# Expert stage of a two-block fp32 model: the last two of 32 expert pairs added from on-chip memory, the others gathered while these two run

## The chip, the cores and the metric

The program runs on one core of one Trainium2 chip, in fp32. The metric is the device time of one execution in microseconds (us). All figures of the trace come from one profiled execution.

## What is computed

The reference is a two-block network on 512 tokens of width 1024. Only its last part matters here: a mixture of 64 experts, two for each token, added to the residual, and a final normalisation.

```python
def _hier_moe(h, wg, bg, we, be, w_gate, w_up, w_down):
    ...
    gate_w = p_g * jax.nn.softmax(top_l, axis=-1)
    expert = g_idx * EXPERTS_PER_GROUP + top_i
    ...
    def expert_block(args):
        xb, e = args
        a = jax.nn.silu(xb @ w_gate[e]) * (xb @ w_up[e])
        return a @ w_down[e]

    y_pad = lax.map(expert_block, (x_pad.reshape(n_blocks, MOE_BLOCK, d), block_e)).reshape(rows, d)
    y = y_pad[dest] * w_s[:, None].astype(h.dtype)
    out = jax.ops.segment_sum(y, tok_s, num_segments=t)
...
        x = x + _hier_moe(hn, router_group_w[i], router_group_b[i], router_expert_w[i],
                          router_expert_b[i], expert_w_gate[i], expert_w_up[i], expert_w_down[i])
    return _rmsnorm(x, final_norm_g)
```

w_gate and w_up are 1024 x 512 for each expert, w_down is 512 x 1024: 6 MB an expert, some 400 MB in all, each read once.

## The kernel before

The engines' programs are written by hand, in the order in which they are to run, with semaphores between them; no scheduler moves anything. PE is TensorE, DVE VectorE, ACT ScalarE, POOL GpSimd, SP SyncE, which issues the weight loads.

The expert stage takes a little over the last third of the span. Experts are taken two at a time, as 32 **pairs**. A pair has 128 slots, 64 for each of its experts, of which on average 32 hold a token. The routing writes two tables: TAB has the token of each slot of a pair, DEST the row of y_d (a DRAM buffer of 1024 rows, one for each token and choice) for its result. An empty slot points outside the buffer and its row is skipped. For pair q:

- POOL gathers the token rows from hn_d (DRAM) into XG[q % 2] (L1893), and PE transposes them (L794). ACT copies the first half of the result to XT (L1162), DVE the second (L1779).
- PE multiplies by the gate weights (L804), 16 products of 64 x 512 results; ACT takes the tanh (L1166), DVE makes the gate from it (L1781). PE multiplies by the up weights (L804 too) and DVE finishes the product (L1784).
- PE transposes that (L811), ACT copies it (L1170), PE multiplies by the down weights (L821). DVE (L1788) and ACT (L1174) copy the two halves to YE, one buffer for all pairs, and POOL scatters YE to y_d (L1897). Pair q's copy waits until the scatter of pair q-1 has landed.

The weights come on SP's queue, 2 MB a load, six loads a pair, into a **ring** of nine slots of 2 MB. A load is issued when PE has ended the product that used its slot before. Slot names: the first four are WR[1], WR[2], WR[3] and WR[0]. PE's results go to eight PSUM banks in turn; a tile opens when the bank's last user has been read.

A general path (`more_rounds`) for experts with more than 64 tokens stands behind the pairs in every engine's program. It is not entered in the profiled execution: each engine loads the number of rounds into a register, compares, and goes on.

After the last scatter has landed, SP reads y_d back in eight loads (L2011), one for each block of 128 tokens and each of the two choices. DVE adds each, times its weight, to the residual X (L1796, 8 combines), ACT squares the rows (L1179) and takes the root (L1181), DVE makes the factor and multiplies the four row blocks by it and the gain `row` (L1800), and SP writes them out (L2014).

Of the kernel before, what the change touches and what calls it, by code (L numbers as in the profile page):

```python
# [14 lines left out]
P = 128  # L15
CAP = 64
PAIRS = 32
NONE = 4096
# [128 lines left out]
def program(nc, A, out):  # L147
    with ExitStack() as ctx:
# [160 lines left out]
        RR, OK, o2 = zl(2, 4), zl(2, 4), zl(2, 4)  # L309
# [13 lines left out]
        YG = [view(zone, ring0 + 1024 * n, 1024) for n in range(8)]  # L323
# [15 lines left out]
        plan += [(("ex", n), RING[n % NRING]) for n in range(6 * PAIRS)]  # L339
        W = Slots(plan)  # L340
        EW = [A[n].rearrange("e (p t) n -> e p (t n)", p=P) for n in ("eg", "eu", "ed")]
# [19 lines left out]
        def tensor_program(pe):  # L361
# [409 lines left out]


            pe_plan(pe, T, any_bank())
            for q in range(PAIRS):
                pe_pair(pe, T, q, lambda n: loaded("ex", 6 * q + n), lambda n: slot("ex", 6 * q + n), any_bank, ("gather", q % 2, 16 * (q // 2 + 1)))
                for n in range(6):
                    W.ended[("ex", 6 * q + n)] = (("g", q), ("g", q), ("u", q), ("u", q), ("d", q, 1), ("d", q, 1))[n]
            pe.wait_ge(S("rounds"), 1)

        def pe_plan(pe, table, b):  # L780
# [4 lines left out]
            ins.then_inc(table.f("tab"), 1)  # L785

        def pe_pair(pe, table, q, ready, weight, bank, gathered):
# [10 lines left out]
            for mat, name in enumerate(("g", "u")):  # L798
                o = open_tile(pe, (name, q), bank(), 1, table)
# [13 lines left out]
            pe.wait_ge(*table.free("at", q))  # L813
            pe.wait_ge(*ready(4))
# [15 lines left out]
        def scalar_program(act):  # L830
# [35 lines left out]
            odd_columns(0, sm("n1"))  # L866
            act.wait_ge(S("lam"), 1)
# [278 lines left out]
            act.wait_ge(S("hn_rows"), 4)  # L1146
            act.dma_start(row, A["fn2"].partition_broadcast(P)).then_inc(S("row"), 16)
# [6 lines left out]

            for q in range(PAIRS):
                act_pair(act, T, q, q % 2)

        def act_pair(act, table, q, par):
# [11 lines left out]
            act.activation(aT, table.ap("at", q).rearrange("p (a b) -> p a b", a=4), ACT.Copy).then_inc(table.s("at", q), 1)  # L1170
            act.wait_ge(*table.full("d", q, 1))
            if q:
                act.wait_ge(S("y_st"), 16 * q)
            act.activation(YE[:, 512:1024], table.ap("d", q, 1), ACT.Copy).then_inc(table.s("d", q, 1), 1)  # L1174

        def act_end(act):
            for i in range(4):
                act.wait_ge(S("comb"), 2 * i + 2)
# [7 lines left out]
        def vector_program(dve):  # L1186
# [564 lines left out]

            for q in range(PAIRS):
                dve_pair(dve, T, q, q % 2)

        def dve_plan(dve, own, table):
# [12 lines left out]
            step(dve.tensor_tensor(OK, OK, ck("tok").rearrange("p (a b) -> p a b", a=2), ALU.mult))  # L1768
            step(dve.tensor_tensor(BM[:, 0, :, :], BM[:, 0, :, :], bc(OK[:, 0, :], 2, 32), ALU.mult))
            dve.tensor_tensor(BM[:, 1, :, :], BM[:, 1, :, :], bc(OK[:, 1, :], 2, 32), ALU.mult).then_inc(S("am"), 1)  # L1770
# [3 lines left out]

        def dve_pair(dve, table, q, par):
            dve.wait_ge(*table.full("xt", q, 1))
            if q > 1:
                dve.wait_ge(*table.full("u", q - 2))
            dve.tensor_copy(XT[par][:, 4:8, :], table.ap("xt", q, 1).rearrange("p (a b) -> p a b", a=4)).then_inc(table.s("xt", q, 1), 1)  # L1779
            dve.wait_ge(S("a_tanh"), q + 1)  # L1780
            dve.scalar_tensor_tensor(AT, AT, 1.0, table.ap("g", q), ALU.add, ALU.mult).then_inc(table.s("g", q), 1)  # L1781
            dve.wait_ge(*table.free("g", q))
            dve.wait_ge(*table.full("u", q))
            dve.scalar_tensor_tensor(AT, AT, 0.5, table.ap("u", q), ALU.mult, ALU.mult).then_inc(table.s("u", q), 1)  # L1784
            dve.wait_ge(*table.full("d", q, 0))
            if q:
# [460 lines left out]
```

## Time and profile before

| | us |
|---|---|
| median of 3 runs | 2759.55 |
| lowest, highest | 2752.46, 2761.93 |
| profiled execution, its time | 2755.31 |
| profiled execution, its span | 2753.5 |
| PE busy (share of the span) | 2396.7 (87%) |
| DVE, ACT, POOL busy | 595.7, 330.1, 161.1 |

The span runs from the first instruction of the program to the last. The profile's page cuts it into 40 slices of 69 us. In the last 14 slices DMA is busy at nine tenths or more and moves some 425 GB/s: the expert weights. In the last slice this falls to four tenths. "PEclk" is the granted clock of TensorE, 1.00 for the full 2.4 GHz and 0.50 for 1.2 GHz. Views used: the chain of waits (what each step of the end waited for), windows (busy time in a stretch), the timeline (instructions in order), groups by line, and the DMA view. A line of the trace is a line of the kernel as printed above.

### The profile page before, as it was taken

The page shows a single profiled execution, that of the slowest core. Times are in us where ns is not written, and L with a number is a line of the kernel's source. Part 1 is how long each engine was busy: PE and PEld are TensorE (multiplying, and loading weights), DVE is VectorE, ACT ScalarE, POOL GpSimd, SP SyncE. Part 2 cuts the span into 40 slices and gives each one's busy share as a digit, 9 for nine tenths or more (in the row PEclk, how much of TensorE's full clock was granted, in tenths as well). Part 3 has the DMA queues.
Part 4 walks back from the last instruction along what each step waited for, and adds up shares of the span by engine and source line. Part 5 has one row for each costly group of instructions (what it writes and reads, how often), then busy time and mean ns, then how long its engine had stood idle before and what let it go on. Part 6 is the DMA issues. An engine that isn't in the chain of part 4 may idle for free.

```text
span 2753.5 us, 20729 instructions
## 1 busy us (share of the span) xinstructions
PE 2396.7 (87%) x8540; PEld 1131.7 (41%) x8540; DVE 595.7 (22%) x1191; ACT 330.1 (12%) x637; POOL 161.1 (6%) x149
## 2 busy tenths in 40 slices
PE   7998989897999999997999998698788878888874
PEld 3654544453444554443564444333233323332331
DVE  1144252523144223002152111211000000010002
ACT  2012122210021110002111000000000000000001
POOL 0000000000004330000000000000000000000000
PEclk9998999898999999998978999799999999999997
DMA  4210000002222322212632223699999999999994
GB/s 181 79 59 31 31 31 31 16 23 99 88 111 93 110 95 85 85 68 74 113 94 92 115 95 131 244 425 426 426 425 426 426 425 426 425 425 414 427 425 180
DMA packets 68416, 549.00 MB, mean 199 GB/s; under 512 B 20961, under 2 KB 25185, under 8 KB 36449
## 3 DMA queue, kind: packets, MB, share of 16 engines
q1 hardware_dynamic: 42384, 518.11, 46.4%
q10 hardware_dynamic: 16720, 21.13, 2.7%
q0 software_dynamic: 9216, 8.42, 0.9%
q8 instruction: 69, 1.13, 0.2%
q14 instruction: 27, 0.21, 0.0%
HBM read 540.76 MB, written 32.01 MB: 208 GB/s over the span
## 4 chain that ended last, share of the span: by engine, by line
PE 61%; DMA 20%; DVE 6%; ACT 2%; issue 1%; ACTq 1%; DVEq 0%; POOL 0%; SPq 0%; POOLq 0%
PE ps L364 23%; DMA sb<-in_eu 14%; PE ps L804 9%; PE ps L643 8%; PE ps L419 6%; DMA sb<-in_eg 5%; PE ps L821 4%; PE ps L538 2%; PE ps L703 1%; PE ps L508 1%; PE ps L530 1%; DMA sb<-in_ed 1%; DVE sb L1190 1%; PE ps L509 1%; DVE sb L1312 1%
## 5 line engine op out<-in xcount | busy, mean ns | idle before, releaser
L364 PE MATMUL ps<-sb 128*128 128x512 f32 (+2 forms) x1920 | 792.8, 575 | 33.5 <-DVE sb L1322 15.3
L804 PE MATMUL ps<-sb 128*64 128x512 f32 x2048 | 495.6, 640 | 116.9 <-DMA sb<-in_eu 87.7
L364 PEld LDWEIGHTS ps<-sb 128*128 128x128 f32 x1920 | 360.5, 195 | 449.4 <-issue 431.0
L804 PEld LDWEIGHTS ps<-sb 128*64 128x64 f32 x2048 | 180.3, 146 | 410.3 <-issue 381.9
L821 PE MATMUL ps<-sb 128*64 128x512 f32 x1024 | 233.6, 610 | 24.9 <-ACT sb L1170 19.9
L419 PE MATMUL ps<-sb 128*128 128x512 f32 x512 | 251.3, 621 | 0.0
L643 PE MATMUL ps<-sb 128*128 128x512 f32 x512 | 220.0, 592 | 0.8 <-ACT sb L856 0.8
L643 PEld LDWEIGHTS ps<-sb 128*128 128x128 f32 x512 | 97.3, 190 | 122.9 <-issue 122.9
L821 PEld LDWEIGHTS ps<-sb 128*64 128x64 f32 x1024 | 73.6, 139 | 162.8 <-issue 136.0
L1190 DVE TENSOR_TENSOR sb<-sb 128x32 f32<-128x32 f32 (+10 forms) x259 | 106.7, 430 | 133.6 <-PE ps L609 83.2
L419 PEld LDWEIGHTS ps<-sb 128*128 128x128 f32 x512 | 93.0, 199 | 80.1 <-issue 79.6
L1784 DVE SCALAR_TENSOR_TENSOR sb<-sb,ps 128x512 f32<-128x512 f32 x32 | 22.1, 690 | 314.9 <-PE ps L804 314.9
L856 ACT ACTIVATE sb<-ps 128x512 f32<-128x512 f32 (+6 forms) x123 | 60.1, 499 | 229.0 <-PE ps L364 92.5
L538 PE MATMUL ps<-sb 128*64 128x128 f32 x320 | 51.8, 295 | 39.3 <-ACT sb L856 25.2
L1897 POOL DMA_INDIRECT y_d<-sb x32 | 32.2, 1007 | 891.5 <-ACT sb L1174 862.8
L1223 DVE COPY sb<-ps 128x512 f32<-128x512 f32 (+7 forms) x65 | 36.5, 561 | 210.7 <-PE ps L364 96.9
L1781 DVE SCALAR_TENSOR_TENSOR sb<-sb,ps 128x512 f32<-128x512 f32 x32 | 22.1, 690 | 255.5 <-ACT sb L1166 255.5
L538 PEld LDWEIGHTS ps<-sb 128*64 128x64 f32 x320 | 35.2, 143 | 83.6 <-issue 33.1
L1170 ACT ACTIVATE sb<-ps 128x512 f32<-128x512 f32 x32 | 19.1, 598 | 389.0 <-PE ps L811 389.0
L371 PE MATMUL ps<-sb 128*128 128x128 f32 x128 | 23.1, 366 | 47.2 <-DVE sb L1213 23.7
L974 ACT ACTIVATE sb<-ps,sb 128x128 f32<-128x128 f32 (+3 forms) x64 | 33.2, 523 | 242.3 <-DVE sb L1397 239.3
L1788 DVE COPY sb<-ps 128x512 f32<-128x512 f32 x32 | 22.2, 693 | 177.8 <-PE ps L821 177.8
(233 smaller groups left out, 1461.2 us busy)
## 6 DMA issues: line engine op xcount, KB each, us to landing
sb<-in_eg SPq DMA_DIRECT2D x64, 2048.0 KB, 32.5
sb<-in_eu SPq DMA_DIRECT2D x64, 2048.0 KB, 34.1
sb<-in_ed SPq DMA_DIRECT2D x64, 2048.0 KB, 32.5
sb<-in_m SPq DMA_DIRECT2D x16, 2048.0 KB, 7.4
sb<-in_winF SPq DMA_DIRECT2D x6, 2048.0 KB, 9.9
sb<-in_mg SPq DMA_DIRECT2D x8, 1536.0 KB, 6.6
sb<-in_mgg SPq DMA_DIRECT2D x4, 2048.0 KB, 7.2
sb<-in_wo SPq DMA_DIRECT2D x4, 2048.0 KB, 7.2
```

Of the source, the lines that this page charges most:

```text
L364: ins = pe.matmul(out, lhsT, rhs, start=k == 0, stop=k == len(pieces) - 1)
L419: ins = pe.matmul(o, lhsT, rhs, start=k == 0, stop=k == 7)
L508: pe.matmul(o[:, 0:nk], qT[hs, j, 128 * i:128 * i + 128], kT[hs, ty, 0:nk], start=True, stop=False)
L538: ins = pe.matmul(ob[hs, 128 * i:128 * i + 128], Vn[:, kb, 128 * ty + 64 * h:128 * ty + 64 * h + 64], PTR[ty][:, 128 * kb:128 * kb + 128], ...
L643: ins = pe.matmul(acc[2 * i + nh], HT[:, k, 128 * i:128 * i + 128], w[:, q, 512 * nh:512 * nh + 512], start=k == 0, stop=k == 31)
L804: ins = pe.matmul(o[64 * e:64 * e + 64, :], x[:, k, 64 * e:64 * e + 64], weight(2 * mat + e)[:, 512 * k:512 * k + 512], start=k == 0, stop ...
L821: ins = pe.matmul(o[64 * e:64 * e + 64, :], aT[:, k, 64 * e:64 * e + 64], weight(4 + e)[:, d:d + 512], start=k == 0, stop=k == 3)
L856: act.activation(dst, T.ap(*name) if src is None else src, ACT.Copy).then_inc(T.s(*name), 1)
L974: act.activation(PR[n % 2][:, ty, 0:nk], T.ap("s", n, ty)[:, 0:nk], ACT.Exp, bias=ST[n % 2][:, ty:ty + 1], scale=0.125, accum_out=ST[n % 2 ...
L1190: return own(dve.tensor_tensor(o, a, b, op))
L1223: dve.tensor_copy(dst, T.ap(*name) if src is None else src).then_inc(T.s(*name), 1)
L1897: pool.indirect_dma_start(out=y_d, out_offset=bass.IndirectOffsetOnAxis(ap=rows, axis=0), in_=YE, in_offset=None, bounds_check=1023, oob_i ...
```

## The change

Pairs 0 to 29 (`ENDS = 30`) still go through y_d. Pairs 30 and 31 do not: their YE is made with the routing weight already in it (WTAB, one column for each), and PE spreads it over the tokens by products with one-hot matrices OH (`pe_spread`: 8 products of 128 x 128 by 128 x 512 a pair, one for each block of 128 tokens and half of the width). DVE adds these to X (`dve_spread`, 8 additions a pair).

The results of the 30 pairs are no longer loaded by SP. POOL gathers them from y_d in eight gathers of 128 rows (GY, the rows' table, leaves out those of pairs 30 and 31), after the scatter of pair 29 has landed; DVE combines six of them behind its XT copy of pair 31, and two behind the up product of pair 31. For their buffers they take WR[1], the two XG and `row`. The gain `row` is thus loaded later: ACT issues that load after the sixth combine. The last 12 loads of weights leave WR[1] out and go round the other eight slots. The two last loads, the down weights of pair 31, are issued as 8 loads of 512 KB, and PE's products with them go by k, both halves of the width together. At the end DVE makes the row blocks 2 and 3, POOL and ACT make blocks 0 and 1. Early in the program, two DMAs on ACT's queue fill y_d with x.

```diff
@@ the ring
-        YG = [view(zone, ring0 + 1024 * n, 1024) for n in range(8)]
+        OH = [view(CKt, 128, 4, 128), view(RW, 0, 4, 128)]
+        YA = [view(WR[1], 1024 * n, 1024) for n in range(4)] + [XG[0], row, XG[1], view(WR[1], 0, 1024)]
...
-        plan += [(("ex", n), RING[n % NRING]) for n in range(6 * PAIRS)]
+        plan += [(("ex", n), RING[n % NRING]) for n in range(6 * ENDS)]
+        plan += [(("ex", n), RING[1 + (n - 6 * ENDS) % (NRING - 1)]) for n in range(6 * ENDS, 6 * PAIRS)]
@@ TensorE
+            o = open_tile(pe, ("wtab",), any_bank())
+            pe.wait_ge(S("bw"), 1)
+            for n in range(8):
+                ins = pe.matmul(o[:, 0:2], AM[:, n // 4, n % 4, :], BW[:, n, :], start=n == 0, stop=n == 7)
...
+        def pe_spread(pe, q, bank):
+            pe.wait_ge(S("oh"), 4 * (q - ENDS) + 4)
+            pe.wait_ge(*T.free("d", q, 0))
+            pe.wait_ge(*T.free("d", q, 1))
+            for i in range(4):
+                for nh in range(2):
+                    o = open_tile(pe, ("sp", q, i, nh), bank())
+                    pe.matmul(o, OH[q - ENDS][:, i, :], YE[:, 512 * nh:512 * nh + 512], start=True, stop=True).then_inc(T.f("sp", q, i, nh), 1)
...
             for mat, name in enumerate(("g", "u")):
+                if q == PAIRS - 1 and mat == 1:
+                    pe_spread(pe, q - 1, bank)
...
+            if q == PAIRS - 1:
+                both = [open_tile(pe, ("d", q, nh), bank(), 1, table) for nh in range(2)]
+                for k in range(4):
+                    for e in range(2):
+                        pe.wait_ge(S(f"last{e}{k}"), 16)
+                    for nh in range(2):
+                        for e in range(2):
...
@@ ScalarE
+            for c in range(2):
+                act.dma_start(y_d[512 * c:512 * c + 512, :], A["x"]).then_inc(S("y_init"), 16)
...
-            act.wait_ge(S("hn_rows"), 4)
-            act.dma_start(row, A["fn2"].partition_broadcast(P)).then_inc(S("row"), 16)
...
             for q in range(PAIRS):
                 act_pair(act, T, q, q % 2)
+                if q == ENDS:
+                    act.wait_ge(S("comb"), 6)
+                    act.dma_start(row, A["fn2"].partition_broadcast(P)).then_inc(S("row"), 16)
...
+            if q == PAIRS - 1:
+                act.activation(e1, e1, ACT.Sqrt, scale=0.0)
...
+            act.wait_ge(S("l_r"), 1)
+            for i in range(2):
+                act.wait_ge(S("gained"), i + 1)
+                act.activation(Z[:, i, :], Z[:, i, :], ACT.Copy, scale=r5[:, i:i + 1]).then_inc(S("fin_a"), 1)
@@ VectorE
+            dve_pair(dve, T, ENDS, 0)
+            q = PAIRS - 1
+            dve_xt(dve, T, q, 1)
+            for n in range(6):
+                dve_comb(dve, n, S("comb"), YA[n], S(f"comb{n}"))
+            dve_gate(dve, T, q)
+            dve_spread(dve, q - 1, own)
+            dve_up(dve, T, q)
...
+            for n in (6, 7):
+                dve_comb(dve, n, S("comb"), YA[n], S(f"comb{n}"))
+            dve_ye(dve, T, q)
+            dve_spread(dve, q, own)
...
+        def dve_spread(dve, q, own):
...
+                    dve.tensor_tensor(xs, xs, T.ap("sp", q, i, nh), ALU.add).then_inc(S("xadd") if q > ENDS else T.s("sp", q, i, nh), 1)
@@ GpSimd
+            pool.wait_ge(S("y_st"), 16 * ENDS)
+            pool.wait_ge(S("gy"), 1)
+            for n in range(8):
...
+                gather(pool, YA[n], y_d, GY[:, n % 2, n // 2:n // 2 + 1], 1023, S(f"comb{n}"))
+            pool.wait_ge(S("xadd"), 8)
...
+        def pool_end(pool):
+            pool.wait_ge(S("row"), 48)
+            for i in range(2):
+                pool.wait_ge(S("l_sq"), i + 1)
+                pool.tensor_tensor(Z[:, i, :], X[:, i, :], row, ALU.mult).then_inc(S("gained"), 1)
@@ SyncE
+            for k in range(4):
+                for e in range(2):
+                    sp.dma_start(slot("ex", 6 * PAIRS - 2 + e)[:, 1024 * k:1024 * k + 1024],
+                                 EW[2][2 * PAIRS - 2 + e][:, 1024 * k:1024 * k + 1024]).then_inc(S(f"last{e}{k}"), 16)
...
-            sp.wait_ge(S("y_st"), 16 * PAIRS)
-            for n in range(8):
-                i, c = n // 2, n % 2
-                sp.dma_start(YG[n], y_d[512 * c + 128 * i:512 * c + 128 * i + 128, :]).then_inc(S(f"comb{n}"), 16)
```

On ACT, around the end of pair 30, before: the four operations of pair 30, then those of pair 31.

```order
L1162 ACTIVATE sb<-ps 128x512 [waits full2,full5]
L1166 ACTIVATE sb<-ps 128x512 [waits full2,full7]
L1170 ACTIVATE sb<-ps 128x512 [waits full4,full1]
L1174 ACTIVATE sb<-ps 128x512 [waits y_st,full3]
L1162 ACTIVATE sb<-ps 128x512 [waits full1,full4]
L1166 ACTIVATE sb<-ps 128x512 [waits full1,full6]
L1170 ACTIVATE sb<-ps 128x512 [waits full3,full0]
L1174 ACTIVATE sb<-ps 128x512 [waits y_st,full2]
```

And now (L1202, L1206, L1210 and L1220 are the same four; in_fn2 is the gain):

```order
L1202 ACTIVATE sb<-ps 128x512 [waits full3,full6]
L1206 ACTIVATE sb<-ps 128x512 [waits full3,full0]
L1210 ACTIVATE sb<-ps 128x512 [waits full5,full2]
L1220 ACTIVATE sb<-ps,sb 128x512 [waits free3,y_st,full4]
L1196 DMA sb<-in_fn2 128x1024 [waits comb]
L1202 ACTIVATE sb<-ps 128x512 [waits full2,full5]
L1206 ACTIVATE sb<-ps 128x512 [waits full2,full7]
L1210 ACTIVATE sb<-ps 128x512 [waits full4,full1]
L1212 ACT_TABLE_LOAD
L1212 ACTIVATE sb<-sb 128x4
L1220 ACTIVATE sb<-ps,sb 128x512 [waits full7,full3]
```

The load of the gain, with its wait on the combines, now stands ahead of ACT's copy to XT of pair 31, and the square root's table is loaded ahead of pair 31's last copy.

On DVE, pair 31 before, from its copy to XT to its copy to YE:

```order
L1779 COPY sb<-ps 128x512 [waits full1,full5]
L1781 SCALAR_TENSOR_TENSOR sb<-sb,ps 128x512 [waits a_tanh]
L1784 SCALAR_TENSOR_TENSOR sb<-sb,ps 128x512 [waits full7,free6]
L1788 COPY sb<-ps 128x512 [waits y_st,full1]
L2071 TENSOR_LOAD sb [waits rounds]
```

And now, from the same copy to the first of the additions for pair 30 (L1835 is a combine, L1903 the gate):

```order
L1899 COPY sb<-ps 128x512 [waits full2,full6]
L1835 SCALAR_TENSOR_TENSOR sb<-sb 128x1024 [waits comb0]
L1835 SCALAR_TENSOR_TENSOR sb<-sb 128x1024 [waits comb,comb1]
L1835 SCALAR_TENSOR_TENSOR sb<-sb 128x1024 [waits comb,comb2]
L1835 SCALAR_TENSOR_TENSOR sb<-sb 128x1024 [waits comb,comb3]
L1835 SCALAR_TENSOR_TENSOR sb<-sb 128x1024 [waits comb,comb4]
L1835 SCALAR_TENSOR_TENSOR sb<-sb 128x1024 [waits comb,comb5]
L1903 SCALAR_TENSOR_TENSOR sb<-sb,ps 128x512 [waits a_tanh]
L1848 TENSOR_TENSOR sb<-sb,ps 128x512 [waits full0,comb]
```

Six combines, each of which waits for its own gather, stand between the copy to XT and the gate of pair 31.

## Rows read from the trace of the kernel before

**Rows 1.** Chain that ended last, from 2600 us: start, duration (us), what.

```profile
2683.55 31.33 DMA sb<-in_ed
...
2723.71 2.60 DMA y_d<-sb
...
2726.33 0.34 SPq L2011
```

**Rows 2.** Windows: stretch, length, busy us (PE, PEld, DVE, ACT, POOL), PEclk, DMA, GB/s.

```profile
2700.00:2710.00 10.00, 8.44 (x41) 3.11 (x39) 0.69 (x1) 0.60 (x1) 0.00 (x0) 1.00 0.30 126
2710.00:2720.00 10.00, 7.91 (x40) 3.32 (x38) 1.38 (x2) 0.60 (x1) 0.00 (x0) 1.00 0.09 38
```

**Rows 3.** Timeline of pair 31: start, duration (us), engine, line, out<-in, [idle before].

```profile
2695.34 0.60 ACT L1162 ACTIVATE sb<-ps 128x512 f32<-128x512 f32 x1
2695.79 0.69 DVE L1779 COPY sb<-ps 128x512 f32<-128x512 f32 x1 [3.82 <-PE ps L794]
...
2696.58 7.09 PE L804 MATMUL ps<-sb 128*64 128x512 f32 x32 [0.83 <-ACT sb L1162]
...
2704.34 0.69 DVE L1781 SCALAR_TENSOR_TENSOR sb<-sb,ps 128x512 f32<-128x512 f32 x1 [7.86 <-ACT sb L1166]
...
2705.23 7.09 PE L804 MATMUL ps<-sb 128*64 128x512 f32 x32 [1.56 <-DMA sb<-in_eu]
...
2712.43 0.69 DVE L1784 SCALAR_TENSOR_TENSOR sb<-sb,ps 128x512 f32<-128x512 f32 x1 [7.40 <-PE ps L804]
...
2714.02 0.60 ACT L1170 ACTIVATE sb<-ps 128x512 f32<-128x512 f32 x1 [9.72 <-PE ps L811]
...
2715.13 7.09 PE L821 MATMUL ps<-sb 128*64 128x512 f32 x32 [1.15 <-DMA sb<-in_ed]
```

**Rows 4.** Timeline of the end.

```profile
2733.32 8.23 DVE L1796 SCALAR_TENSOR_TENSOR sb<-sb 128x1024 f32<-128x1024 f32 x6 [0.60 <-DMA sb<-y_d]
...
2741.58 1.06 ACT L1179 ACTIVATE sb<-sb 128x1024 f32<-128x1024 f32 x1 [1.63 <-DVE sb L1796]
...
2742.75 1.28 ACT L1181 ACT_TABLE_LOAD   x1
...
2745.29 4.87 DVE L1800 SCALAR_TENSOR_TENSOR sb<-sb 128x1024 f32<-128x1024 f32 x4
2746.60 3.92 SPq L2014 DMA_DIRECT2D out<-sb  x4
```

**Rows 5.** Timeline of POOL: a scatter to y_d, a gather from hn_d.

```profile
2664.08 1.01 POOL L1897 DMA_INDIRECT y_d<-sb  x1 [29.46 <-ACT sb L1174]
...
2665.39 1.02 POOL L1893 DMA_INDIRECT sb<-hn_d,sb  x1 [0.31 <-issue]
```

**Rows 6.** DMA view from 2660 us: issues, count, median us from issue to landing.

```profile
y_d<-sb POOLq DMA_INDIRECT x3, 10.1
sb<-hn_d,sb POOLq DMA_INDIRECT x1, 14.3
```

**Rows 7.** Page, part 3: a queue's packets, MB, share of 16 DMA engines, whole span.

```profile
q0 software_dynamic: 9216, 8.42, 0.9%
```

**Rows 8.** DMA view of 2640 to 2664 us: all packets.

```profile
DMA packets 876, 10.15 MB, mean 423 GB/s; under 512 B 230, under 2 KB 230, under 8 KB 265
```

**Rows 9.** DMA view of 2731 to 2739 us: q1's packets, MB, share of 16 engines.

```profile
q1 hardware_dynamic: 807, 2.92, 91.6%
```

**Rows 10.** Windows, TensorE after an idle stretch: the columns of rows 2.

```profile
1762.20:1768.00 5.80, 4.91 (x16) 2.69 (x18) 0.69 (x1) 0.60 (x1) 0.00 (x0) 0.50 0.09 26
```

**Rows 11.** Windows, TensorE at the start: length, PE busy us (count), PEclk, DMA share, GB/s.

```profile
22.50:75.40 52.90, 52.90 (x124) 1.00 0.18 72
```

**Rows 12.** Source view of L2071, register load of the rounds: durations (ns), start.

```profile
L2071 POOLq TENSOR_LOAD <-sb x1: 475/475/475, 2726.3 to 2726.3; - x1
```

**Rows 13.** Groups by line, POOL: line, op, out<-in (shapes) xcount | busy us, mean ns.

```profile
L1845 POOL TENSOR_TENSOR sb<-sb 128x512 f32<-128x512 f32 x32 | 48.8, 1525 | 22.1 <-DVE sb L1554 14.5 <-DVE sb L1558 7.6
L1832 POOL TENSOR_TENSOR sb<-sb 128x512 f32<-128x512 f32 x32 | 33.3, 1039 | 224.7 <-ACT sb L1015 224.7
```

More of the change, by code:

```diff
@@ L17 @@
 PAIRS = 32
+ENDS = 30
 NONE = 4096
@@ L1749, in vector_program @@
             dve_plan(dve, own, T)
-            for q in range(PAIRS):
-                dve_pair(dve, T, q, q % 2)
+            flat8 = HI.rearrange("p a b -> p (a b)")
+            after(tt(o2, OK, WT, ALU.mult))
+            after(tt(BW, bc(ck("iota")[:, ENDS:PAIRS], 1, 8), bc(flat8, 2, 2), ALU.is_equal))
+            dve.tensor_tensor(BW, BW, bc(o2.rearrange("p a b -> p (a b)"), 2, 2), ALU.mult).then_inc(S("bw"), 1)
+            dve_rows(dve, own, ENDS)
+            copy(("wtab",), WTAB, T.ap("wtab")[:, 0:2])
@@ L1755, in dve_plan, with dve_hots @@
+        def dve_hots(dve, own):
+            dve.wait_ge(*T.full("rank"))
+            dve.wait_ge(*T.full("lg"))
+            dve.wait_ge(*T.free("tab"))
+            dve.wait_ge(own.sem, own(dve.tensor_copy(TOKF, TAB[:, ENDS:PAIRS])))
+            for p in range(2):
+                for i in range(4):
+                    dve.tensor_scalar(OH[p][:, i, :], ck("iota"), TOKF[:, p:p + 1], -128.0 * i, ALU.subtract, ALU.is_equal).then_inc(S("oh"), 1)
         def dve_plan(dve, own, table):
@@ L1880, in gpsimd_program @@
             pool.wait_ge(S("hn"), 16)
-            for q in range(PAIRS + 2):
+            for q in range(PAIRS):
+                if q == 2:
+                    pool.wait_ge(S("y_init"), 32)
                 if q > 1:
@@ L1997, in sync_program @@
                     sp.wait_ge(*T.full("lg"))
-                load(("ex", n), EW[k // 2][2 * q + k % 2])
+                if n < 6 * PAIRS - 2:
+                    load(("ex", n), EW[k // 2][2 * q + k % 2])
+            for e in range(2):
+                sp.wait_ge(*T.full(*W.ended[W.before[("ex", 6 * PAIRS - 2 + e)]]))
+            for k in range(4):
+                for e in range(2):
+                    sp.dma_start(slot("ex", 6 * PAIRS - 2 + e)[:, 1024 * k:1024 * k + 1024],
+                                 EW[2][2 * PAIRS - 2 + e][:, 1024 * k:1024 * k + 1024]).then_inc(S(f"last{e}{k}"), 16)
         def sync_more(sp):
@@ L2067, in meet, with nothing, more_rounds @@
                 eng.sem_clear(S("go" + letter))
-        def more_rounds(eng, letter, more, pair):
+        def nothing(eng):
+            pass
+        def more_rounds(eng, letter, more, pair, tail=nothing):
             eng.wait_ge(S("rounds"), 1)
@@ L2083, in more_rounds @@
                     eng.reg_add(k, k, 1)
+                tail(eng)
+                meet(eng, letter)
                 eng.reg_add(r, r, 1)
```

141 lines of the change are left out of this document (111 added, 30 removed).

## The prediction, made before the changed kernel was run

> **What bounds the kernel now.** I read the chain that ended last first, for what holds the end; then the windows of the last pair, for who is busy; then the timeline, for the hand-offs that the change moves. The chain says that the pairs hang on their weights: the last load is issued at 2683.55 and lands 31.33 us later, at 2714.9 [rows 1]. The windows refine this. From 2700 to 2710 the 16 DMA engines are only 0.30 busy, from 2710 to 2720 only 0.09 [rows 2]: most engines have ended and a few still carry their share of the last loads. A load has landed only when the slowest engine has done its part. I call these the slow engines; everything new that is put on them before 2714.9 counts. Behind the weights come 7.1 us of down products, a scatter, the reads of y_d, six combines in 8.23 us and the final normalisation [rows 1, 3, 4], 31 us from the end of the last product to the end of the span. The change goes at this tail.
>
> **Removed.** The last scatter and the reads of y_d, from 2723.71 on [rows 1], and the combines behind them, up to 2741.55 [rows 4]. Most of this goes to other places, so I don't subtract it; I lay out the new end from pair 31 on and compare the ends.
>
> **What comes ahead of pair 31's gate products.** PE needs both copies to XT. DVE's is unmoved. ACT's (0.60 us [rows 3]) now stands behind the load of the gain, which waits for six combines, and these for six gathers. So the question of the case is when the sixth gather lands.
>
> The scatter of pair 29 is issued at 2664.08 and lands about 10.1 us later, at 2674.1; the gather behind it, issued at 2665.39, takes 14.3 us, to 2679.7 [rows 5, 6]. That is 5.6 us for one indirect DMA whose rows are mostly empty. It has 9216 / 64 = 144 packets, 9 for each DMA engine [rows 7]. A 16 KB packet of weights takes 16384 B over 423 / 16 GB/s = 0.62 us [rows 8], and 9 x 0.62 = 5.6: each packet of POOL's queue waits out one packet of SP's. The Trainium skill ("DMA: Bandwidth & Descriptors", section "Queues, rings and completion order") has each engine alternate between its queues, a whole packet of some 9 to 17 descriptors at a time; the 5.6 us fit turns of either length, and both give the same landing here.
>
> The eight new gathers are full: their rows are 4 KB, and a 4 KB packet takes 0.16 us (2.92 MB / 807 packets over 365 GB/s / 0.916 / 16 [rows 9]). 15 rows in 16 belong to the 30 pairs, so a gather costs a loaded engine 9 x 0.62 + 7.5 x 0.16 = 6.8 us. They are issued from 2674.2, one in 1.3 us [rows 5], and queue behind the gather that lands at 2679.7. If all weights came in 16 KB packets, the sixth would land at 2679.7 + 6 x 6.8 = 2720.4, which is the late bound. But the last two loads now come in 4 KB packets. At 2679.7 a slow engine has 35.2 / 0.62 = some 56 packets of weights left; 40 of them stay at 16 KB and take 40 x 0.62 + 33 x 0.16 = 30.1 us with the packets in between, to 2709.8. By then 40 of the 54 packets of six gathers are through; the last 14 alternate with 4 KB packets, 14 x 0.31 = 4.3 us. **The sixth gather lands at 2714.1.** The early bound comes from DVE: it starts to combine after its XT copy, at 2696.5, and six combines at 8.23 / 6 = 1.37 us [rows 4] end at 2704.7. I take 2714.1, since the 5.6 us are measured under the very same load; both bounds stay for the range.
>
> **The path from there.** Sixth combine to 2715.4; issue of the gain's load (0.34 to 0.4, like SP's issue [rows 1]) and ACT's copy 0.6, with hand-offs 2716.6. PE starts the gate products there and not at 2696.58 [rows 3]: 20.0 us later.
> - Gate products 7.09 us at full clock. PE has been idle for 20 us by then. After an idle stretch the granted clock was 0.50 from 1762.2 to 1768.0, with PE busy [rows 10]; half of 5.8 us is lost, 2.9 (bounds: 0, and 7.1 if all of it runs at 1.2 GHz). To 2726.6.
> - Spread of pair 30, 8 products. A product of 128 x 128 by 128 x 512 takes 52.90 / 62 = 0.85 us at full clock (two records each) [rows 11]: 6.8 us, to 2733.4. Its eighth tile takes the bank of the gate products, which DVE frees in time (tanh and gate, from 2703.67 to 2705.03, take 1.4 us [rows 3]). DVE's eight additions, 0.7 us each like L1784, run beside it.
> - Up products 7.1, to 2740.5. Then L1784, transposes, L1170: 2712.32 to 2714.62, 2.3 us [rows 3], to 2742.8. The two remaining combines and the root's table lie under what follows.
> - Down products 7.1, to 2749.9. The weights don't hold them: the slow engines carry at most 8 gathers x 1.3 us = 10.2 us more than before, so the last part lands by 2725. The finer loads are thus worth nothing here; with the old order they would have been worth up to three quarters of 7.1 us.
> - Scaled copy 0.7; spread of pair 31, 6.8; last addition 0.7: 2758.1.
> - The last square, 1.06 and its read 0.19, is one way on; then the table (still loaded: the program has a table load between squares and root on this path too), root and DVE's small steps, 2742.75 to 2745.29, to 2761.9; two final products on DVE at 1.2 us [rows 4] to 2764.3. The other way is POOL. It waits for the eighth addition, loads the number of rounds (0.5 us for the load itself [rows 12]; I take 1 us with the branch) and makes two products of 128 x 1024. Its 128 x 512 ones take 1.04 to 1.53 us [rows 13], so 2.1 to 3.1 each; at 2.5 it ends at 2764.1, and ACT's scaling, 1.06 as for a square [rows 4], at 2765.2. POOL is the later. The last write is issued there.
> - Before, the last final product ended at 2750.16 (2745.29 + 4.87 [rows 4]) and the span at 2753.5: 3.3 us. New end 2768.5, **15 us later**.
>
> **At nothing.** The 8 MB of traffic that fill y_d: at 423 GB/s [rows 8] 20 us, when PE is busy all of 52.90 us and DMA at 0.18 [rows 11]; without that cover a load that PE waits for would come up to 20 us late. The nine small DVE steps and eight products behind the routing: they run while the first gather is under way, some 3.4 us of cover, and could cost 1 us. One slot less for the last 12 loads: a load waits 32 us or so in the queue [rows 1], a slot is 5; only fast engines run dry, and no one waits for those. The one-hot matrices, eight small DVE steps in pair 2: DVE idles 7 us and more at a time [rows 3].
>
> **Rivals.**
> - *Early gathers.* The sixth gather lands before DVE wants it; the combines end at 2704.7 and all follows 10.7 us sooner: span 2757.9, 4.4 us over before, which is no difference that can be told. For it: twelve of the 16 engines have spare time [rows 2], and the slow ones may give POOL's queue more turns. Against: 5.6 us for nine nearly empty packets [rows 6, 7]. It decides at a landing of 2707: sooner than that, the loss is under 0.3%. The Trainium skill (the same page, section "Anatomy of one DMA — SWDGE (gpsimd) path") gives about 2.0 us plus the bytes over 436 GB/s for a DMA from GpSimd, some 3.2 us for 512 KB; by that all six are in by 2684, which is this rival. The trace shows that figure only on idle queues (2.60 us for a scatter [rows 1]), not under the weights (10.1 [rows 6]).
> - *Late gathers.* The 4 KB loads give no extra turns: 2720.4, 6.3 us more, span 2774.8.
> - *Faster.* ACT's copy would go ahead without the combines, as if the gain's load stood elsewhere. Gate products at 2696.6, spread to 2710.5, up to 2717.6, down from 2719.9 to 2727.0, then as above 18.6 us: 2745.6, 8 us less. Against it stands the order of ACT, and DVE's gate is behind the same combines. Only if the gathers were in by 2700 and the additions cheaper than I think is anything of it left.
>
> **The numbers.** My forecast 0.56, late gathers 0.20, early 0.20, faster 0.04. From the profiled execution (2755.31, of which 2753.5 span) the forecast is +15.0. The median of the runs stands 4.2 us above that execution; I add to the median: 2759.6 + 15.0 = 2774.6. Early gathers give 2764.0, late ones 2780.9. With the clock (-2.9 to +4.2), POOL's products (1 us either way) and the spread of the runs, the range is 2760 to 2784. About 0.3%, 8.3 us, is what a measurement of this kernel can tell from no change. Forecast and late case lie above, but the forecast's low flank reaches it: slower 0.76. Early gathers and that flank: same 0.20. Faster 0.04.
>
> **What would show it.** In the profile after: PE idle between the transposes of pair 31 and its gate products, some 20 us, ended by ACT's copy; DVE's fourth to sixth combine each waiting for its gather, 3 to 7 us apart; gathers from y_d with 12 to 35 us to landing; the down products of pair 31 back to back, with no wait for in_ed. Wrong would be: combines back to back at 1.37 us from 2696 on (early gathers), a gap of 25 us and more (late), gate products that start before the sixth combine (the path is not the one I laid out), or a pace of the earlier pairs that has changed.

## The result, and the profile after

The kernel before took 2756.24 us (median of 6 runs, 2751.08 to 2761.93), the changed kernel 2772.45 us (6 runs, 2770.28 to 2776.36). The ratio is 1.0061 with a 95% interval of 1.0045 to 1.0077: **16.2 us slower**, about twice what a measurement can tell. Forecast was +15.0 us and 2774.6 us, range 2760 to 2784. (The forecast added to the 2759.55 us of the first three runs of the kernel before; with six its median is 3.3 us lower.) The profiled execution of after took 2771.85 us, its span is 2770.1 (before 2753.5).

The first view is again the chain that ended last, from the scatter of pair 29 on (start, duration in us, what):

```profile
2662.09 10.31 DMA y_d<-sb
...
2679.63 30.96 DMA sb<-y_d,sb
...
2710.62 1.30 DVE sb L1835
...
2711.93 0.36 ACTq L1196
...
2712.39 0.61 ACT sb L1202
...
2713.05 9.73 PE ps L828 x32
2722.78 7.07 PE ps L807 x16
...
2739.24 7.12 PE ps L846 x32
```

Before, the chain at this place was a load of weights that landed at 2714.9 and then the scatter and the reads of y_d [rows 1]. Now it is the scatter of pair 29, a gather that takes 30.96 us to land, the sixth combine (L1835), the issue of the gain's load (L1196), ACT's copy to XT (L1202) and the products of pair 31. No weights stand in it.

The timeline shows the same hand-offs with the idle time before each (columns as in rows 3):

```profile
2694.23 4.06 DVE L1835 SCALAR_TENSOR_TENSOR sb<-sb 128x1024 f32<-128x1024 f32 x3
...
2702.57 1.28 DVE L1835 SCALAR_TENSOR_TENSOR sb<-sb 128x1024 f32<-128x1024 f32 x1 [4.28 <-DMA sb<-y_d,sb]
2708.11 1.28 DVE L1835 SCALAR_TENSOR_TENSOR sb<-sb 128x1024 f32<-128x1024 f32 x1 [4.25 <-DMA sb<-y_d,sb]
2710.62 1.28 DVE L1835 SCALAR_TENSOR_TENSOR sb<-sb 128x1024 f32<-128x1024 f32 x1 [1.23 <-DMA sb<-y_d,sb]
...
2712.39 0.60 ACT L1202 ACTIVATE sb<-ps 128x512 f32<-128x512 f32 x1 [19.17 <-DVE sb L1835]
...
2713.05 9.73 PE L828 MATMUL ps<-sb 128*64 128x512 f32 x32 [19.46 <-ACT sb L1202]
...
2739.24 7.10 PE L846 MATMUL ps<-sb 128*64 128x512 f32 x32 [0.69 <-ACT sb L1210]
```

Three combines find their rows there, three wait for a gather each. ACT idles 19.17 us before its copy, PE 19.46 us before the gate products, which started at once in [rows 3] (0.83 us, at 2696.58). The down products (L846) wait 0.69 us, for ACT, where they waited 1.15 us for in_ed before.

The windows of the same stretch (columns of rows 2):

```profile
2700.00:2710.00 10.00, 0.00 (x0) 0.00 (x0) 2.57 (x2) 0.00 (x0) 0.00 (x0) 0.50 0.64 253
2710.00:2720.00 10.00, 6.96 (x20) 2.14 (x22) 1.28 (x1) 0.60 (x1) 0.00 (x0) 0.58 0.37 150
```

In [rows 2] PE was busy 8.44 us of the first ten; now it does nothing there, and the clock granted is 0.50, the lower of the two levels (1.2 GHz). DMA is busier than before, 0.64 in place of 0.30: the gathers share the engines with the last weights. The DMA view from 2662 to 2700 us answers [rows 6]:

```profile
sb<-y_d,sb POOLq DMA_INDIRECT x8, 19.7
y_d<-sb POOLq DMA_INDIRECT x1, 10.3
sb<-hn_d,sb POOLq DMA_INDIRECT x1, 14.4
```

And the timeline of the end, which answers [rows 4]:

```profile
2756.46 1.28 ACT L1228 ACT_TABLE_LOAD   x1
...
2756.52 4.63 POOL L2070 TENSOR_TENSOR sb<-sb 128x1024 f32<-128x1024 f32 x2 [58.76 <-ACT sb L1226]
...
2757.99 0.18 DVE L1935 RECIPROCAL sb<-sb 128x4 f32<-128x4 f32 x1 [1.35 <-ACT sb L1228]
2758.21 0.67 DVE L1936 TENSOR_TENSOR sb<-sb 128x4 f32<-128x4 f32 x1
2758.91 2.26 DVE L1938 TENSOR_TENSOR sb<-sb 128x4 f32<-128x4 f32 x1
...
2761.61 2.19 ACT L1232 ACTIVATE sb<-sb 128x1024 f32<-128x1024 f32 x2 [3.65 <-DVE sb L1940]
2761.61 2.48 DVE L1926 SCALAR_TENSOR_TENSOR sb<-sb 128x1024 f32<-128x1024 f32 x2
2762.92 1.53 SPq L2176 DMA_DIRECT2D out<-sb  x2
2764.51 1.36 SPq L2179 DMA_DIRECT2D out<-sb  x2
```

**How the traces are compared from here on.** The scatter of pair 29 starts at 2664.08 before and at 2662.09 after, and elsewhere in the experiments too (2662.08 in e1, 2666.68 in e2): executions drift by a few us ahead of the stretch that matters. The pairs themselves are not changed, from the first gather of rows to this scatter it is 905.3 us before and 905.4 after. So I count from the start of that scatter in each trace. Before ends 89.4 us behind it (2753.5 - 2664.1), after 108.0 (2770.1 - 2662.1): 18.6 us more, of which the 2.0 us by which the scatter came sooner are to be taken off to get the difference of the two spans, 16.6. In the eleven traces of this study the scatter starts between 2661.0 and 2668.4, so these 2.0 us can't be laid to the change. Medians of runs decide on the size; the trace says where it lies.

### The profile page after: what moved, and what is told of

It reads as the page before. It is cut to its first block, busy times and chain, and to the rows that moved or that the text cites. A ratio compares the mean times of both kernels' runs of the same rounds, so it can differ in the third digit from the quotient of the medians.

```text
span 2770.1 us, 20900 instructions
## 1 busy us (share of the span) xinstructions
PE 2420.0 (87%) x8588; PEld 1144.4 (41%) x8588; DVE 609.9 (22%) x1223; ACT 335.4 (12%) x642; POOL 172.7 (6%) x157
## 3 DMA queue, kind: packets, MB, share of 16 engines
q8 instruction: 70, 1.15, 0.2%
## 4 chain that ended last, share of the span: by engine, by line
PE 62%; DMA 19%; DVE 6%; ACT 2%; issue 2%; ACTq 1%; POOL 0%; DVEq 0%; POOLq 0%
PE ps L371 22%; DMA sb<-in_eu 13%; PE ps L828 10%; PE ps L650 8%; PE ps L426 6%; PE ps L858 5%; DMA sb<-in_eg 2%; PE ps L545 2%; PE ps L710 1%; PE ps L515 1%; PE ps L537 1%; DMA sb<-in_ed 1%; DMA sb<-y_d,sb 1%; DVE sb L1241 1%; PE ps L516 1%
## 5 line engine op out<-in xcount | busy, mean ns | idle before, releaser
L371 PE MATMUL ps<-sb 128*128 128x512 f32 (+2 forms) x1920 | 790.6, 573 | 32.6 <-DVE sb L1373 15.3
L1241 DVE TENSOR_TENSOR sb<-sb 128x32 f32<-128x32 f32 (+11 forms) x261 | 107.0, 428 | 133.8 <-PE ps L616 83.2
L1903 DVE SCALAR_TENSOR_TENSOR sb<-sb,ps 128x512 f32<-128x512 f32 x32 | 22.1, 690 | 260.9 <-ACT sb L1206 260.9
L1210 ACT ACTIVATE sb<-ps 128x512 f32<-128x512 f32 x32 | 19.1, 598 | 368.2 <-PE ps L835 368.2
```

Of the source, the lines that this page charges most:

```text
L371: ins = pe.matmul(out, lhsT, rhs, start=k == 0, stop=k == len(pieces) - 1)
L1241: return own(dve.tensor_tensor(o, a, b, op))
```

## The experiments

My theory: two orders of instructions make the loss. ACT's load of the gain, with its wait for six combines, stands ahead of ACT's copy to XT; and on DVE the six combines stand ahead of the gate. Both hang on the sixth gather, which is late because it shares the DMA engines with the weights. Rival one: the loss is in the weights themselves, which the gathers push back. Rival two: it is in the new work on the path (16 products that spread, 16 additions, the POOL and ACT share of the last step), and the wait would be hidden without them.

### The gain's load behind pair 31 (e1_gain_last)

```diff
-                if q == ENDS:
-                    act.wait_ge(S("comb"), 6)
-                    act.dma_start(row, A["fn2"].partition_broadcast(P)).then_inc(S("row"), 16)
...
+            act.wait_ge(S("comb"), 6)
+            act.dma_start(row, A["fn2"].partition_broadcast(P)).then_inc(S("row"), 16)
```

The added lines stand behind the last step of pair 31 on ACT; nothing else is changed.

> The load of the gain is issued behind all of ACT's work for pair 31; all else as in the changed kernel. My theory: ACT's copy to XT waits on the six combines only through this load. Gate products start at about 2694.4 in place of 2713.05 and end near 2701.5; then DVE's gate, behind the sixth combine, becomes the wait (2712.6), the eighth tile of the spread follows, up products 2713.4 to 2720.5. That is 16 us less: about 2756 us, span about 2754. Rival, the slow engines' weights hold the end anyway: then less than 5 us are won, and PE waits for in_ed.

Measured: 2757.11 us (median of 10), ratio to the kernel before 1.0009 [0.9993, 1.0025]; **15.3 us less than the changed kernel**, where 16 were expected. From the scatter to the end 93.2 us in place of 108.0. The timeline of PE and DVE:

```profile
2693.87 7.09 PE L828 MATMUL ps<-sb 128*64 128x512 f32 x32 [2.39 <-DMA sb<-in_eg]
...
2709.25 1.28 DVE L1834 SCALAR_TENSOR_TENSOR sb<-sb 128x1024 f32<-128x1024 f32 x1 [1.09 <-DMA sb<-y_d,sb]
2710.45 0.68 DVE L1902 SCALAR_TENSOR_TENSOR sb<-sb,ps 128x512 f32<-128x512 f32 x1
...
2711.19 2.08 PE L807 MATMUL ps<-sb 128*128 128x512 f32 x2 [4.02 <-DVE sb L1902]
2713.20 8.91 PE L828 MATMUL ps<-sb 128*64 128x512 f32 x32
```

The gate products no longer wait for the combines, only 2.39 us for their weights, and take 7.09 us, at full clock. Now the second order bites: the gate (L1902) follows the sixth combine, the last two products of the spread wait 4.02 us for it, and the up products take 8.91 us in place of 7.09 because PE had stood still (granted clock 0.79 from 2713.2 to 2722.1). So the wait on ACT costs 15 us net of what the second wait takes back. Rival two falls: all the new work is still there. Rival one falls as the main cause: by it less than 5 us could be won, and the down products wait 0.69 us for ACT, not for weights.

### DVE's combines behind the gate (e2_combines_late)

The gain's load as in the run before, and on DVE:

```diff
-            for n in range(6):
-                dve_comb(dve, n, S("comb"), YA[n], S(f"comb{n}"))
...
+            for n in range(6):
+                dve_comb(dve, n, S("comb"), YA[n], S(f"comb{n}"))
```

The removed lines stand ahead of the gate of pair 31, the added ones behind the step that follows its up products; the additions of pair 30 no longer wait for the combines, those of pair 31 do.

> As e1_gain_last, and DVE makes the gate, the additions of pair 30 and the up product of pair 31 first, then combines 0 to 5, the scaled copy, combines 6 and 7. My theory: no one in pair 31 waits for a gather any more. Gate products to 2701.5, spread to 2708.5, up products to 2715.6, down products held by their last parts (about 2723) to 2725; last addition 2734.5, end near 2749: 21 us less than the changed kernel, 2751 to 2752 us, and 4 to 5 below the kernel before. Rival, DVE's combines only move and become the wait ahead of the copy to YE: no more than e1_gain_last, 2756.

Measured: 2752.20 us (10), ratio 0.9983 [0.9970, 0.9995], where 2751 to 2752 us were expected; from the scatter to the end 86.2 us, 7.0 less than e1. In the timeline PE has no gap from the gate products to the end of the up products, and the six combines run back to back, since all rows are in by then:

```profile
2698.55 7.09 PE L828 MATMUL ps<-sb 128*64 128x512 f32 x32 [2.38 <-DMA sb<-in_eg]
2705.57 7.14 PE L807 MATMUL ps<-sb 128*128 128x512 f32 x16
...
2712.64 7.09 PE L828 MATMUL ps<-sb 128*64 128x512 f32 x32
...
2720.45 8.23 DVE L1835 SCALAR_TENSOR_TENSOR sb<-sb 128x1024 f32<-128x1024 f32 x6
```

The books close in the traces: 108.0 - 14.8 - 7.0 = 86.2, against 89.4 before. **The two waits cost 21.8 us, and what the change takes off the tail is worth 3.2 us net of the work it adds.** What remains of rival one is the 2.38 us wait for in_eg ahead of the gate products; [rows 3] had 0.83 there, for ACT. Counted from the scatter, though, the gate products start no later than before: at 31.9 us, and at 32.5 in the kernel before.

That the gathers are late because of the weights shows in the eighth of this run. It is issued when nearly all weights have landed (SP's queue takes 4.6% of the engines' time from 2722 to 2724), and lands in 4.6 us, where the sixth, the same 512 KB, took 29.2:

```profile
sb<-y_d,sb POOLq DMA_INDIRECT x1, 4.6
```

### The last two loads whole (e3_whole_loads)

The changed kernel with its last two loads in one 2 MB piece each, as before. PE waits for both whole loads ahead of the down products instead of for each piece; all other waits stay:

```diff
-                for e in range(2):
-                    sp.dma_start(slot("ex", 6 * PAIRS - 2 + e)[:, 1024 * k:1024 * k + 1024],
-                                 EW[2][2 * PAIRS - 2 + e][:, 1024 * k:1024 * k + 1024]).then_inc(S(f"last{e}{k}"), 16)
+                load(("ex", n), EW[k // 2][2 * q + k % 2])
```

> The two last loads of weights are again 2 MB each, in 16 KB packets, all else as in the changed kernel. If POOL's queue gets one packet for each packet of SP's, the sixth gather lands later: from 4.3 us for 14 turns beside 4 KB packets to 14 x 0.62 + 13 x 0.16 = 10.8, so 6 us later (2716 to 2717 in place of 2710.6), and the time is 5 to 6 us more, about 2778. If the engines share by bytes, the landing and the time don't change.

Measured: 2778.62 us (4), ratio 1.0081 [1.0064, 1.0098], 6.2 us more than the changed kernel in the medians; 3.0 more from the scatter to the end of the profiled one. The combines in its timeline:

```profile
2700.70 1.28 DVE L1836 SCALAR_TENSOR_TENSOR sb<-sb 128x1024 f32<-128x1024 f32 x1 [2.16 <-DMA sb<-y_d,sb]
2705.97 1.28 DVE L1836 SCALAR_TENSOR_TENSOR sb<-sb 128x1024 f32<-128x1024 f32 x1 [3.99 <-DMA sb<-y_d,sb]
2711.96 1.28 DVE L1836 SCALAR_TENSOR_TENSOR sb<-sb 128x1024 f32<-128x1024 f32 x1 [4.70 <-DMA sb<-y_d,sb]
2717.98 1.28 DVE L1836 SCALAR_TENSOR_TENSOR sb<-sb 128x1024 f32<-128x1024 f32 x1 [4.74 <-DMA sb<-y_d,sb]
```

The gathers land 5.3, 6.0 and 6.0 us apart to the end, where in the changed kernel the sixth came 2.5 us behind the fifth. Counted from the scatter the sixth combine starts 52.8 us later here (2717.98 - 2665.18), 48.5 in the changed kernel (2710.62 - 2662.09): 4.3 us sooner by the finer loads, two thirds of the 6.3 that I had worked out. At the end 3.0 of them are left, because the gate products, behind 25.18 us of idle time, took 8.56 us here and 9.73 in the changed kernel. The finer loads help the gathers, and through them the kernel, though they were not cut for that.

### All final products on DVE (e4_dve_final)

The changed kernel, with the four final products on DVE as before and none on POOL and ACT:

```diff
-            for i in (2, 3):
+            for i in range(4):
...
-                pool_end(pool)
```

> The four final products are all on DVE again and are written out in the order of before; no work on POOL and no scaling on ACT at the end. In the changed kernel's trace two small DVE steps of 128 x 4 took 0.67 and 2.26 us while POOL ran its product, against 0.16 before. If POOL's products hold DVE, the two steps are back at 0.16 to 0.2, 2.6 us are won and 2.4 us of two more final products are lost, and ACT's 1.1 us behind them go: 0 to 1.5 us less, 2771 to 2772. If not, the steps stay slow and the time is 1 to 3 us more.

Measured: 2772.04 us (4), ratio 1.0057 [1.0040, 1.0074]: by the medians of four and six runs no difference from the changed kernel can be told. The traces tell one: from the last addition to the end 12.0 us here and in e10 below, and 14.8 or 14.9 in all five traces with POOL's share (after, e1, e2, e3, e7). Its timeline:

```profile
2760.62 0.16 DVE L1932 TENSOR_TENSOR sb<-sb 128x4 f32<-128x4 f32 x1
2760.81 0.16 DVE L1934 TENSOR_TENSOR sb<-sb 128x4 f32<-128x4 f32 x1
...
2761.41 4.87 DVE L1922 SCALAR_TENSOR_TENSOR sb<-sb 128x1024 f32<-128x1024 f32 x4
2762.72 3.92 SPq L2172 DMA_DIRECT2D out<-sb  x4
```

The two small DVE steps take 0.16 us each; with POOL's products beside them they took 0.67 and 2.26, which is 2.6 of the 2.8 us. The run takes ACT's products away together with POOL's, but ACT's start only when these steps have ended, so they can't be what held them. Sharing the last step among three engines is a loss, not a gain.

### Whole loads without the two waits (e7_late_whole)

e2 with the last two loads whole, the edit of e3, its wait of PE for both loads too.

> e2_combines_late with the two last loads whole again. If finer loads are worth what the prediction's text gave them once nothing else holds the down products: the second whole load lands at about 58 us after the scatter of pair 29 (2722.9 in e3_whole_loads at 2665.2 for the gathers that end with it), the down products start there and not at 55.4: 2 to 3 us slower than e2_combines_late, about 2754.5 us. If the engines' queues are done before, no difference.

Measured: 2754.95 us (10), ratio 1.0001 [0.9990, 1.0013]; 2.75 us more than e2, but the two were run beside other runs of the kernel before (medians 2755.20 and 2754.26). From the scatter to the end 87.0 against 86.2. Its down products wait for the load:

```profile
2720.11 7.11 PE L847 MATMUL ps<-sb 128*64 128x512 f32 x32 [1.33 <-DMA sb<-in_ed]
```

With the two waits gone the finer loads take this 1.33 us down to 0.69, a wait for ACT; they are worth 0.8 us in the traces; the medians say 2.8, but the intervals of the two ratios overlap. In the changed kernel they did nothing for the down products, which came 16 us behind the last weights.

### The parts put together, and the gathers held back (e5_best, e8_gathers_later)

e5 is e2 and e4 together, and the spread and the last down products in the other order, half a row first, so that the squares can start sooner:

```diff
-                for k in range(4):
-                    for e in range(2):
-                        pe.wait_ge(S(f"last{e}{k}"), 16)
-                    for nh in range(2):
+                for nh in range(2):
+                    for k in range(4):
+                        for e in range(2):
+                            if nh == 0:
+                                pe.wait_ge(S(f"last{e}{k}"), 16)
```

> e2_combines_late and e4_dve_final together, and the down products of pair 31 again one half of the width after the other, so that the first half's scaled copy and its spread can start while the second half is multiplied. From the scatter of pair 29 to the end the profile of before has 89.4 us, of e2_combines_late 86.2. My theory: the final products on DVE take 2.8 us off (14.8 to 12.0 from the last addition to the end, as in e4_dve_final), the halves 0.9: 82.4, 7 us under the kernel before, about 2748 us, ratio 0.9975. Rival, the end hangs on the last weights' landing (2723.3 in e2_combines_late): the halves win nothing and the down products wait 1 to 2 us, 84.5, ratio 0.998 to 0.999.

Measured: 2752.53 us (12), ratio 0.9993 [0.9984, 1.0001], 85.9 us from the scatter: missed by some 4 us. The way from the last addition to the end took 12.6, not less than the 12.0 of e4: the squares of all rows fall together behind the last half. And the last addition came at 73.3 us, after 71.4 in e2, since pair 31 as a whole came later: its gate products waited for their weights until 34.4 us and not 31.9. Up to there e5 and e2 run the same code, so this is the spread between two executions. The next run asked whether the gathers are what holds the weights. It is e5 with one wait moved:

```diff
-                    pool.wait_ge(*T.full("u", ENDS - 2))
+                    pool.wait_ge(*T.full("xt", ENDS + 1, 1))
```

POOL now issues the gathers from y_d only when pair 31 has been transposed, some 19 us later.

> e5_best with the first gather from y_d held until the transposes of pair 31 have ended, some 17 us later, so that the slow engines do the weights for the gate and up products of pair 31 first. If the gathers only take turns from the weights: gate products start 2.4 us sooner (PE waited so long for in_eg in e2_combines_late), all weights land at the same time as before or 1 us sooner, the sixth combine ends some 10 us later, near the scaled copy: 0 to 2 us less than e5_best. Rival, the combines now hold the scaled copy: 2 to 5 us more than e5_best.

Measured: 2748.20 us (12), ratio 0.9979 [0.9966, 0.9991], 83.4 us from the scatter. The gate products start at 30.3 us with a shorter wait (34.4 in e5, 31.9 in e2). But the halves now show their price, since the first half of the down products needs every piece of both loads:

```profile
2692.79 7.09 PE L831 MATMUL ps<-sb 128*64 128x512 f32 x32 [1.50 <-DMA sb<-in_eg]
...
2720.94 4.51 PE L850 MATMUL ps<-sb 128*64 128x512 f32 x20 [1.46 <-DMA sb<-in_ed]
```

### The gathers held back, rows in the order of the change (e8_again, e10_later_rows)

The same kernel once more, and beside it e10, which is e2 and e4 with the gathers held back and without the halves.

> The same kernel as e8_gathers_later, to set beside e10_later_rows on one chip: 83.4 us from the scatter of pair 29 to the end, ratio to the kernel before 0.998. If its first result owed more than 2 us to the chip or the moment, it comes out at 0.999 or above.

> e8_gathers_later with the down products, the spread and the additions of pair 31 again in the changed kernel's order (by k, then by row block). In e5_best the squares of all four row blocks bunched behind the last four additions and cost 0.6 us (12.6 from the last addition to the end, 12.0 in e4_dve_final), and the halves won 0.7 us between down products and spread. So both should cancel: within 1 us of e8_gathers_later's 83.4 us from the scatter of pair 29 to the end, about 2748.5 us. If the last weights hold the down products (e8_gathers_later waited 1.5 us for in_ed after three eighths of them), the order by k waits later and less: 1 us better.

Measured: e8_again 2750.49 us (12), ratio 0.9984 [0.9974, 0.9994], 83.2 us from the scatter; e10 2749.06 us (12), ratio 0.9980 [0.9967, 0.9993], 82.0 us, 1.2 to 1.4 less than the kernel with the halves, as expected of weights that hold the down products. The two can't be told apart by their times. Both are faster than the kernel before by about 0.2%, with intervals clear of 1, in e8's first result as well, though this is less than the 0.3% that the prediction gave a single comparison. Against the changed kernel it is 0.8%. The timeline of e10:

```profile
2691.47 7.09 PE L828 MATMUL ps<-sb 128*64 128x512 f32 x32 [1.52 <-DMA sb<-in_eg]
...
2715.01 7.10 PE L846 MATMUL ps<-sb 128*64 128x512 f32 x32 [0.69 <-ACT sb L1209]
```

The down products need not wait for weights, and the wait ahead of the gate products is down from 2.38 (e2) to 1.52 us. e10 ends 4.2 us sooner from the scatter than e2: 1.4 up to the last addition (70.0 us and 71.4), and 2.8 behind it (12.0 and 14.8), POOL's share of the last step. The 1.4 us stand at the start of the gate products already: 30.0 to 30.5 us in the three traces with the gathers held back, 31.8 to 34.4 in the four with early gathers whose gate products wait for weights (e1, e2, e5, e7). The groups don't overlap, but the second spreads by 2.6 us of itself.

## Why the prediction was right, point by point

Each step of the forecast's sum, counted from the start of pair 29's scatter (2664.08 in the forecast, 2662.09 in the trace of after), in us:

| Step | Forecast | Measured |
|---|---|---|
| scatter of pair 29 landed | 10.1 | 10.3 |
| sixth gather landed | 50.0 | 48.5 |
| gate products start | 52.5 | 51.0 |
| gate products, length | 10.0 | 9.73 |
| spread of pair 30 | 6.8 | 7.07 |
| up products | 7.1 | 7.04 |
| to the down products | 2.3 | 2.35 |
| last addition done | 94.0 | 93.2 |
| from there to the end of the span | 10.4 | 14.8 |
| end | 104.4 | 108.0 |

- **The path** is the one laid out: ACT's copy behind the gain's load behind six combines behind six gathers. PE idles 19.46 us (some 20 were forecast), ended by ACT's copy. e1 takes this one wait away and gets 15.3 us back, so it is shown, not argued.
- **The landing of the sixth gather** was 1.5 us off. The DMA view, asked for each issue by itself, gives the landings: 22.0, 28.1, 34.3, 40.4, 45.9 and 48.5 us behind the scatter, after the gather from hn_d at 15.7. The mis-sized term is the pace of a gather under 16 KB packets, put at 6.8 us; it was 6.1 to 6.2 for the first four, and 6.1 on average in e3 (16.0 to 52.8 us). Eight turns of 0.62 us and the 1.2 us of own packets make 6.2, nine don't: a fit, no proof. So nearly five gathers were through, not four and a half, when the 4 KB packets came, and these had less left to speed up. That gathers land faster beside 4 KB packets of weights is borne out: 2.6 us between the fifth and the sixth here, 6.1 in e3 without such packets, and 2.2 to 3.5 us from one to the next of the seven in e10 that are issued when the fine loads are already queued. That POOL's queue gets its turns packet for packet fits this, and no run separates it from the engines having less to do at the end. This is why the rival of late gathers fell. Early gathers fell by the waits of 4.28, 4.25 and 1.23 us.
- The rule that speaks for early gathers, in the Trainium skill ("DMA: Bandwidth & Descriptors", section "Anatomy of one DMA — SWDGE (gpsimd) path"), about 2.0 us and the bytes over 436 GB/s, gives an estimated 3.2 us for such a gather. By that rule, the trace disagrees: the median is 19.7 us with the weights under way, and the slowest 31.0; the nearest to that figure is the 4.6 us of e2's eighth gather.
- **The clock** after the idle time: 2.6 us lost on the gate products (9.73 against 7.09 in e1), 2.9 forecast. The price isn't a steady one: 2.4 us in e4 (9.46, after 20.22 us of idle time) and 1.5 in e3 (8.56, after 25.18).
- **The failed step is the last one**, from the last addition to the end: 10.4 forecast, 14.8 measured, 4.4 us short. In the forecast's own terms: the last final product ended 8.8 us behind the last addition and not 7.1, and the span 6.0 behind that and not 3.3. Two things lie under these numbers. First, POOL. I took its products (2.5 us each; they took 2.31) as a way of their own beside DVE's. But they hold DVE: the step of 128x4 at L1936 ends as POOL's first product does, at 2758.88 (2756.52 + 4.63 / 2 = 2758.84), and that at L1938 with the second, at 2761.17 (2756.52 + 4.63 = 2761.15). Everything behind it, DVE's and ACT's products alike, starts at 2761.61. e4 gives the price, 2.8 us. The Trainium skill has the rule ("SBUF — State Buffer", section "SBUF: two separate sides"): VectorE and GpSimd share a port pair, and a VectorE instruction with two SBUF inputs and a GpSimd instruction that reads SBUF exclude each other: whichever starts first has the ports for its whole length. By that rule, the trace agrees, down to the reciprocal at L1935, which has one input, falls beside the first product and takes 0.18 us as always. The forecast put nothing for this. The load of the root's table stands on the path as said (1.28 us at 2756.46), so the early one that the change puts ahead of pair 31's last copy (2739.21) buys nothing: between the two a table is loaded for the squares (2747.47).
- Second, the writes. I carried over 3.3 us from the last final product to the end. The rows show that the end goes by the *first* write: before, it is issued at 2746.60 and the span ends 6.9 us later; after, at 2762.92 and 7.2; in e4 at 2762.72 and 7.0. The four writes are 2.10 MB and keep the 16 engines busy for 47.4% of the 11 us from 2760 to 2771, that is 5.2 us, at some 400 GB/s (the DMA view of that stretch, after; columns as in rows 9):

```profile
q1 hardware_dynamic: 576, 2.10, 47.4%
```

  The forecast had the first write 5.0 us behind the last addition; with 6.9 behind it the sum would have been 11.9, beside e4's 12.0. The missing 1.5 us are this, the other 2.8 POOL.
- **What made up for it.** The tail was 4.4 us too short, the part before it 0.8 too long, and the scatter came 2.0 us sooner, a drift: +16.6 in the spans, +16.2 in the medians, for +15.0. So part of the closeness is luck: from the scatter on the change costs 18.6 us, 3.6 more than forecast. The middle of the path holds to within 1.5 us at each step, and that is no luck.
- **At nothing** held. The fill of y_d runs beside PE without a gap; in the window at the start PE is busy all of it, with DMA at 0.39 and not at 0.18 [rows 11]:

```profile
22.00:76.00 54.00, 54.00 (x127) 23.94 (x126) 7.75 (x33) 3.68 (x6) 0.00 (x0) 1.00 0.39 153
```

  A kernel without the fill wasn't tried, so this rests on the trace alone. The products behind the routing do lie in the cover of the first gather:

```profile
1756.40 3.55 PE L784 MATMUL ps<-sb 128*128 128x2 f32 x16 [1.08 <-DVE sb L1806]
1760.12 1.97 PE L816 MATMUL ps<-sb 128*128 128x128 f32 x8 [0.17 <-DMA sb<-hn_d,sb]
```

- **The finer loads** "worth nothing here": right for the down products of this kernel, 0.69 us of wait and not for weights. Not the whole of it: e3 shows 3.0 us in the traces and 6.2 in the medians, by way of the gathers. I had that in the sum of the landing and not under the loads.
- **The second wait**, DVE's gate behind the combines, I named only against the rival of a faster kernel, as a reason that it would not come. It is worth 7.0 us in the traces and 4.9 in the medians (e1 to e2). My price for that rival, a span of 2745.6, is 81.5 us from the scatter; e10, with both waits gone, POOL's share gone and the gathers held back, comes to 82.0. e2 alone, 86.2, is 4.7 above it: 4.4 of that is the same tail.

## What to carry to other kernels

Read a queue from its head: a small DMA issue whose only fault is that it waits (here the load of a gain) still holds everything that stands behind it on its engine, and it can go last at no cost, as e1 shows. Work that waits for a DMA under a saturated queue belongs behind the steps that TensorE waits for; priced at its quiet cost it looks free. And before the last step of a kernel is shared among engines, ask what ends it: here the first write did, and the second engine slowed the first.

## What the runs showed that was not expected

- POOL products of 128x1024 hold two-input DVE steps of 128x4 until they end: 0.67 and 2.26 us in place of 0.16.
- The end of the span stands 6.9 to 7.2 us behind the issue of the first of four 512 KB writes in all eleven traces of this study, whether the writes are issued within 3.0 us (after) or 3.9 (e4).
- The eight loads of 512 KB took SP 23.58 us to issue, and 19.0 to 23.5 us in the other runs that have them, where the two whole loads of e3 took 0.80. No run shows what held SP, and nobody waited for it in this time.

```profile
2679.04 23.58 SPq L2163 DMA_DIRECT2D sb<-in_ed  x8
```

- A gather of 512 KB from y_d takes 30.96 us to land in the chain and 19.7 in the median, and 4.6 us when the weights are nearly through. The early gathers push the weights of pair 31 back by little: its gate products waited 2.4 us for in_eg with the gathers issued early (e1, e2) and 1.5 with them late (e8, e10).
